# Hybrid decoder layer with a mixture of experts: routing in batches of 4, 2 and 3 tiles, and the overflow tables computed ahead of the first expert rows

## The chip, the cores and the metric

The kernel runs on one core of a Trainium2 chip. The metric is the device time of one launch in microseconds; lower is better. The engines are named as the profile names them: PE (tensor engine, with PEld its weight loads), DVE (vector engine), ACT (scalar engine), POOL (GpSimd) and SP (sync engine, which here only issues DMA).

## The reference, cut to what matters

One layer of a decoder for 1024 prompt tokens and 8 sample tokens, in float32. A mixer (attention, gated spatial unit, dilated attention, pooling) is followed by a norm, and then by the part that the change touches:

```python
def moe(x, w_router, b_router, w1_l, w3_l, w2_l):
    scores = jax.nn.sigmoid(xt @ w_router)
    sel = scores + b_router
    # best group of 4 experts by the sum of its top two, then the top two experts inside it
    ...
    gate = (jax.nn.one_hot(eidx, N_EXPERTS) * gw[..., None]).sum(1)
    for e in range(N_EXPERTS):          # 16
        h = jax.nn.silu(xt @ w1_l[e]) * (xt @ w3_l[e])
        out = out + gate[:, e:e + 1] * (h @ w2_l[e])
```

with x + MoE(x) normed again. Each token goes to two of 16 experts.

## The kernel before, in words

The tokens are nine tiles s = 0 to 8: tile 0 has the 8 sample tokens, tiles 1 to 8 have 128 prompt tokens each. The mixer ends with an output projection of each tile on PE (`y_half`, matmuls of L460 to L462), after which DVE norms it (`normed`, L839 to L852) into `acc`; ACT helps with one square root (L664). SP stores each normed tile to the DRAM array `yd`.

Routing goes in three batches of tiles, `BATCHES`. For a tile, PE transposes the normed rows (`x1_transposes`, recorded at the helper's line L1205), ACT evicts them (`evict_x1T`, L645) and PE multiplies by the router's weights (`logits`, L522). For a batch, ACT takes the sigmoid of all its logits (`scores`, L655 and L657, with another activation table than the square root), DVE picks the two experts of each token (`choose`, L879 to L912; it signals `mask` after L893), PE counts tokens ahead of each token with the same expert (`positions`, L531 and L532), and DVE turns counts into slots (`place`, L921 to L935, which signals `near`). The logits of a batch lie in one of two PSUM banks, batches 0 and 2 in the same.

Each expert owns 128 "near" slots in the DRAM array `xs`. POOL writes rows to them with indirect DMAs (L1056, `slotS`), two for each tile, and waits for `near` of the batch first. Tokens beyond 128 of an expert go to "far" slots, in 16 overflow tiles that are dealt to experts by the counts: `overflow` (L940 to L955, signals `routed`) works out which expert an overflow tile belongs to and whether it is used at all, `far_slots` (L960 to L969 with L931 to L935, signals `far`) the slots, and POOL then scatters again (L1056, `slotO`, 18 more DMAs).

The expert stage runs over 32 tiles q of 128 slots (`QUEUE`: experts 0 to 7, then overflow tiles and experts in turns, then overflow tiles). For a tile SP loads the rows `xg` (L384; for tile 0 it waits until all near scatters have landed, L412), the weights w1 and w3 in two halves m = 2q and 2q + 1 (`w13_raw`, L371), and w2 (L375). The load of w2 for tile 1 waits for `routed`, and everything behind it on SP's queue waits with it. ACT rounds a weight half (`w13_high`, L678) and DVE takes the rest (`w13_low`, L987), so that a float32 product is made of three matmuls. PE does, in this order: `hidden(q+1)` (24 matmuls, L460 to L462, 12 for each weight half), `x_transposes(q+2)` (L1205), `down(q)` (8 matmuls, L593), `h_transposes(q+1)` (L1205). ACT and DVE split the transposed rows (`rows_high` L687, `rows_low` L995 to L1001), make the product of the hidden layer (`silu` L694, `times` L1010) and scale the result by the gates (`out_low` L708, `out_high` L1017). POOL adds the result into `yd` with an accumulating indirect DMA (`add_rows`, L1073). An add starts only when the add before it has landed, and `out_low(q)` and `out_high(q)` wait until add q - 2 has landed. After the last add SP reads `yd` back, and ACT and DVE do the second norm.

Of the kernel before, what the change touches and what calls it, by code (L numbers as in the profile page):

```python
# [24 lines left out]
NT = SEQ // P  # L25
# [40 lines left out]
def build(nc, a):  # L66

    ctx = ExitStack()
    with ctx:
# [166 lines left out]
        WORDER = RORDER  # L236
        BATCHES = ((0, 4), (4, 7), (7, 9))
        DX = D + 4
# [217 lines left out]
        def emit_pe2(pe, mm, tr):  # L456
# [61 lines left out]
            def logits(s):  # L518
                r = rows(WORDER[s])
                pe.wait_ge(S("x1T"), s + 1)  # L520
                for k in range(KD):
                    m = mm(ps[0:r, 6 + batch_of(s) % 2, s * NE:(s + 1) * NE], x1T[:, k, 0:r], wr[:, k, :],  # L522
                           start=(k == 0), stop=(k == KD - 1))
                m.then_inc(S("lg"), 1)
# [13 lines left out]
            for s in range(2, NT + 1):  # L538
# [4 lines left out]
                if s == 7:  # L543
                    pe.wait_ge(S("rc"), 112)
                    positions(0)
            x1_transposes(NT - 1)
            logits(NT - 1)
            positions(1)
            x1_transposes(NT)
# [59 lines left out]
        def emit_act2(act):  # L609
# [50 lines left out]
            for s in range(NT + 1):  # L660
# [6 lines left out]
                if s == 5:  # L667
                    scores(0)
            scores(1)
            evict_x1T(NT - 1)  # L670
# [42 lines left out]
            rows_high(0)  # L713
            rows_high(1)
            silu(0)
            h_evict(0)
            w13_high(3)
            for q in range(NQ):
# [26 lines left out]
        def emit_dve2(dve, link, last_norm):  # L745
# [225 lines left out]
            for s in range(NT + 1):  # L971
# [5 lines left out]
                if s == 6:  # L977
                    place(0)
            choose(1)
            place(1)  # L980
# [39 lines left out]
            w13_low(1)  # L1020
            w13_low(2)
            rows_low(0)
            rows_low(1)
            times(0)
            overflow()
            w13_low(3)
            for q in range(NQ):
                if q + 2 < NQ:
                    w13_low(2 * q + 4)
                if q + 1 < NQ:  # L1030
                    times(q + 1)
                if q + 2 < NQ:
                    rows_low(q + 2)
                    w13_low(2 * q + 5)
                out_high(q)
                if q == 0:
                    far_slots()

# [13 lines left out]
        def emit_pool2(pool):  # L1052
# [24 lines left out]
            for s in range(NT + 1):  # L1077
                for c in range(2):
                    scatter("slotO", s, c, SLOTS - 1, "scat_far")
                if s == 0:  # L1080
                    pool.wait_ge(S("xd"), 16 * (NT + 1))
                if s % 4 == 0:
                    add_rows(s // 4)
            for q in range(3, NQ):
                add_rows(q)
# [1066 lines left out]
```

## Time and profile before

| | |
|---|---|
| median of 3 runs | 1567.37 us (1563.78 to 1569.9) |
| the profiled execution | 1567.51 us, its span 1565.7 us |
| PE busy | 1419.9 us (91%) |
| DVE busy | 743.7 us (47%) |
| ACT busy | 432.2 us (28%) |
| POOL busy | 309.0 us (20%) |
| DMA | 237.70 MB, mean 152 GB/s |

The routing ends and the expert stage begins about three quarters into the span. There are 32 groups of eight matmuls of L593, one for each expert tile, the first at 1195 us. Times in the rows below are microseconds from the span's start. In a timeline a row is one instruction or a run of like ones; the bracket is how long the engine was idle before it and who released it.

### The profile page before, as it was taken

Reading aid. Unit: us, or ns where it says so; the run is one execution under the profiler, and the core shown is the slowest. Engines: PE = TensorE matmul, PEld = TensorE weight load, DVE = VectorE, ACT = ScalarE, POOL = GpSimd, SP = SyncE. Lnnn points to the kernel's source line nnn. Section 1 sums busy time; section 2 is a strip of 40 time slices with the busy share of each in tenths; the row PEclk is TensorE's granted clock in tenths of the full one; section 3 lists DMA queues with packets and bytes.
Section 4 is the critical chain, followed back from the end, with each engine's and each line's share of the span. In section 5 each row is a group of like instructions: output and inputs, shape, how many; then the busy total and the mean of one; then the engine's idle time right before and its main releaser. Section 6 shows DMA issues by size and latency. Waiting matters only on the chain.

```text
span 1565.7 us, 20000 instructions
## 1 busy us (share of the span) xinstructions
PE 1419.9 (91%) x7544; PEld 1068.0 (68%) x7544; DVE 743.7 (47%) x1302; ACT 432.2 (28%) x721; POOL 309.0 (20%) x233
## 2 busy tenths in 40 slices
PE   7999978799998899999999999999938799999980
PEld 3466465444454599999999999878736466666650
DVE  1266445422124442243443444455666466777746
ACT  1111134201015411111111111212124455665536
POOL 1138920045174000000000000000231521221220
PEclk9969999999999999999999999999958899999995
DMA  7346630255331022232222332422376999888645
GB/s 219 104 134 222 207 127 1 71 172 186 132 99 42 35 77 72 77 104 77 73 93 77 106 142 77 145 78 81 120 300 256 312 302 305 289 300 272 202 164 221
DMA packets 75196, 237.70 MB, mean 152 GB/s; under 512 B 17029, under 2 KB 27476, under 8 KB 61422
## 3 DMA queue, kind: packets, MB, share of 16 engines
q1 hardware_dynamic: 48630, 160.73, 28.4%
q0 software_dynamic: 17792, 59.20, 12.8%
q10 hardware_dynamic: 8704, 16.84, 3.1%
q8 instruction: 43, 0.70, 0.2%
q14 instruction: 27, 0.22, 0.0%
HBM read 213.49 MB, written 65.74 MB: 178 GB/s over the span
## 4 chain that ended last, share of the span: by engine, by line
PE 75%; DMA 8%; DVE 6%; POOL 4%; ACT 3%; issue 3%; SPq 0%; POOLq 0%; DVEq 0%; ACTq 0%
PE ps L460 15%; PE ps L462 14%; PE ps L461 14%; PE ps L1224 11%; DMA tmp_yd<-b,b 7%; PE ps L1205 5%; PE ps L593 4%; POOL b L1967 3%; PE ps L1321 2%; PE ps L1358 2%; PE ps L1409 1%; ACT b L1590 1%; PE ps L522 1%; PE ps L1221 1%; PE ps L1239 1%
## 5 line engine op out<-in xcount | busy, mean ns | idle before, releaser
L460 PE MATMUL ps<-b,b 128*128 128x344 f32 (+1 forms) x1360 | 470.3, 346 | 9.3 <-DVE b L987 3.8
L461 PE MATMUL ps<-b,b 128*128 128x344 f32 (+1 forms) x1360 | 465.8, 342 | 0.0
L462 PE MATMUL ps<-b,b 128*128 128x344 f32 (+1 forms) x1360 | 465.8, 342 | 0.0
L460 PEld LDWEIGHTS ps<-b,b 128*128 128x128 f32 x1360 | 255.2, 188 | 30.8 <-issue 10.7
L462 PEld LDWEIGHTS ps<-b,b 128*128 128x128 f32 x1360 | 255.1, 188 | 19.4 <-issue 0.9
L461 PEld LDWEIGHTS ps<-b,b 128*128 128x128 f32 x1360 | 255.0, 188 | 17.0 <-issue 0.6
L1224 PE MATMUL ps<-b,b 128*128 128x512 f32 (+1 forms) x640 | 258.1, 561 | 0.0
L1224 PEld LDWEIGHTS ps<-b,b 128*128 128x128 f32 x640 | 122.3, 194 | 121.7 <-issue 117.1
L1056 POOL DMA_INDIRECT tmp_xs<-b,b x36 | 44.9, 1247 | 634.4 <-issue 574.9
L1205 PE MATMUL ps<-b,b 128*128 128x128 f32 (+1 forms) x782 | 122.8, 286 | 51.0 <-DMA b<-tmp_xs 18.6
L987 DVE TENSOR_TENSOR b<-b,b 128x2048 fp32r<-128x2048 f32 x64 | 146.3, 2289 | 45.3 <-ACT b L678 42.7
L1205 PEld LDWEIGHTS ps<-b,b 128*128 128x128 f32 (+1 forms) x782 | 93.2, 146 | 101.8 <-issue 48.3
L622 ACT ACTIVATE b<-ps,b 128x344 f32<-128x344 f32 x96 | 52.6, 548 | 379.4 <-PE ps L462 379.4
L593 PE MATMUL ps<-b,b 128*128 128x512 f32 x256 | 117.1, 601 | 9.9 <-ACT b L708 9.4
L776 DVE TENSOR_TENSOR b<-b,ps 128x344 f32<-128x344 f32 x72 | 36.9, 513 | 181.8 <-PE ps L462 181.8
L678 ACT CAST b<-b 128x2048 fp32r<-128x2048 f32 x64 | 122.4, 1917 | 0.0
L1073 POOL DMA_INDIRECT tmp_yd<-b,b x32 | 66.2, 2067 | 226.5 <-DMA tmp_yd<-b,b 199.4
L1967 POOL TENSOR_TENSOR b<-b,b 128x2048 f32<-128x2048 f32 (+1 forms) x24 | 87.8, 3657 | 37.2 <-DMA b<-in_state_k 23.0
L593 PEld LDWEIGHTS ps<-b,b 128*128 128x128 f32 x256 | 46.9, 193 | 57.4 <-issue 56.7
L1801 DVE CUSTOM_DVE_ANT_0 b<-ps,b 128x128 f32<-128x128 f32 (+7 forms) x64 | 45.9, 755 | 49.9 <-PE ps L1321 25.1
L1580 ACT ACTIVATE b<-b,b 128x128 f32<-128x128 f32 (+7 forms) x64 | 49.8, 778 | 21.1 <-DVE b L1801 21.1
L1590 ACT COPY b<-ps 128x512 f32<-128x512 f32 (+3 forms) x64 | 32.1, 502 | 78.1 <-PE ps L1205 78.0
(265 smaller groups left out, 1261.9 us busy)
## 6 DMA issues: line engine op xcount, KB each, us to landing
b<-in_w SPq DMA_DIRECT2D x96, 1024.0 KB
b<-in_w_merge SPq DMA_DIRECT2D x32, 640.5 KB, 4.5
tmp_xs<-b ACTq DMA_DIRECT2D x32, 514.0 KB, 4.0
b<-tmp_xs SPq DMA_DIRECT2D x32, 514.0 KB
b<-in_w_in SPq DMA_DIRECT2D x8, 1024.0 KB, 8.6
b<-in_xT SPq DMA_DIRECT2D x4, 1024.0 KB, 12.4
b<-in_w_out SPq DMA_DIRECT2D x4, 1024.0 KB, 7.7
b<-in_x SPq DMA_DIRECT2D x8, 512.0 KB, 4.0
```

Of the source, the lines that this page charges most:

```text
L460: mm(out, hi, mhi, start=start, stop=False)
L461: mm(out, hi, mlo, start=False, stop=False)
L462: return mm(out, lo, mhi, start=False, stop=stop)
L593: m = mm(ps[:, 2 + c, :], hT[:, u, f, :], w2[q % 3][:, f, c * 512:(c + 1) * 512], start=(f == 0), stop=(f == 1))
L622: act.activation(sg[:, j % 2, :], ps[:, (j % 2) * 2, 0:CH], ACT.Sigmoid, bias=bias).then_inc(S("sgd"), 1)
L678: act.copy(w13_hi[m % 3][:].rearrange("p k n -> p (k n)"), w13_raw[m % 4][:].rearrange("p k n -> p (k n)")).then_inc(S("w13h"), 1)
L987: dve.tensor_tensor(lo, raw, hi.bitcast(F32), ALU.subtract).then_inc(S("w13l"), 1)
L1073: pool.indirect_dma_start(a["yd"], bass.IndirectOffsetOnAxis(rt["to"][:, q % 8:q % 8 + 1], 0), yo[:, u, :], None, bounds_check=TOK - 1, oo ...
L1205: return nc.tensor.transpose(out, in_, ident[0:n, 0:n])
L1224: m = mm(ps[:, j % 2, 0:cw], xT[:, k, t * P:(t + 1) * P], w_ring[:, n % 2, k, 0:cw], start=(k == 0), stop=(k == KD - 1))
L1580: act.activation(p_, p_, ACT.Exp, scale=-1.0, bias=am[:, n % 8:n % 8 + 1], accum_out=asum[:, n % 8:n % 8 + 1]).then_inc(S("ex"), 1)
L1967: pool.tensor_tensor(out, k, q, ALU.mult).then_inc(S("kq"), 1)
```

## The change

Six edits. (1) The batches become 4, 2 and 3 tiles in place of 4, 3 and 2. (2) PE does `positions(1)` ahead of the logits of tile 7, and, since tile 6 now shares its PSUM bank with batch 0, waits for `near` of batch 0 before tile 6's logits. (3) ACT takes the scores of batch 1, and DVE does `choose(1)`, after tile 7's norm and ahead of tile 8's. (4) DVE does `overflow` and `far_slots` after the first three weight halves, ahead of `rows_low(0)`. (5) The fourth weight half, m = 3, is split before `silu(0)` and `times(0)`, no more behind them. (6) POOL issues all 18 far scatters before the first add; before, one add stood behind the second and one behind the tenth of them.

```diff
--- before.py
+++ after.py
@@ -234,7 +234,7 @@
         prod = at(BI + 256 + 8 * CH, [P, CH])
 
         WORDER = RORDER
-        BATCHES = ((0, 4), (4, 7), (7, 9))
+        BATCHES = ((0, 4), (4, 6), (6, 9))
         DX = D + 4
 
         wo_raw = [at(OT, [P, KD, 512]), at(XT, [P, KD, 512])]
@@ -518,6 +518,8 @@
             def logits(s):
                 r = rows(WORDER[s])
                 pe.wait_ge(S("x1T"), s + 1)
+                if s == BATCHES[2][0]:
+                    pe.wait_ge(S("near"), 1)
                 for k in range(KD):
                     m = mm(ps[0:r, 6 + batch_of(s) % 2, s * NE:(s + 1) * NE], x1T[:, k, 0:r], wr[:, k, :],
                            start=(k == 0), stop=(k == KD - 1))
@@ -544,8 +546,8 @@
                     pe.wait_ge(S("rc"), 112)
                     positions(0)
             x1_transposes(NT - 1)
+            positions(1)
             logits(NT - 1)
-            positions(1)
             x1_transposes(NT)
             logits(NT)
             positions(2)
@@ -666,7 +668,8 @@
                     merged_high(s + 3)
                 if s == 5:
                     scores(0)
-            scores(1)
+                if s == 7:
+                    scores(1)
             evict_x1T(NT - 1)
             evict_x1T(NT)
             scores(2)
@@ -712,9 +715,9 @@
             w13_high(2)
             rows_high(0)
             rows_high(1)
+            w13_high(3)
             silu(0)
             h_evict(0)
-            w13_high(3)
             for q in range(NQ):
                 if q + 2 < NQ:
                     w13_high(2 * q + 4)
@@ -976,7 +979,8 @@
                     choose(0)
                 if s == 6:
                     place(0)
-            choose(1)
+                if s == 7:
+                    choose(1)
             place(1)
             choose(2)
             place(2)
@@ -1019,11 +1023,12 @@
             w13_low(0)
             w13_low(1)
             w13_low(2)
+            overflow()
+            far_slots()
             rows_low(0)
             rows_low(1)
+            w13_low(3)
             times(0)
-            overflow()
-            w13_low(3)
             for q in range(NQ):
                 if q + 2 < NQ:
                     w13_low(2 * q + 4)
@@ -1033,8 +1038,6 @@
                     rows_low(q + 2)
                     w13_low(2 * q + 5)
                 out_high(q)
-                if q == 0:
-                    far_slots()
 
             def finish(s):
                 r = rows(WORDER[s])
@@ -1077,11 +1080,8 @@
             for s in range(NT + 1):
                 for c in range(2):
                     scatter("slotO", s, c, SLOTS - 1, "scat_far")
-                if s == 0:
-                    pool.wait_ge(S("xd"), 16 * (NT + 1))
-                if s % 4 == 0:
-                    add_rows(s // 4)
-            for q in range(3, NQ):
+            pool.wait_ge(S("xd"), 16 * (NT + 1))
+            for q in range(NQ):
                 add_rows(q)
 
         block = ctx.enter_context(nc.Block())
```

POOL's whole program from the first scatter on. `tmp_xs` is `xs`, `tmp_yd` is `yd`; the second operand of a scatter is `slotS` (b_137664) or `slotO` (b_137760).

```order
-L1056 DMA tmp_xs<-b_99072_151,b_137664_213 4096x1028 x18
-L1056 DMA tmp_xs<-b_99072_151,b_137760_214 4096x1028 x2
-L1073 DMA tmp_yd<-b_82464_170,b_137920_216 1032x1024
-L1056 DMA tmp_xs<-b_99072_151,b_137760_214 4096x1028 x8
-L1073 DMA tmp_yd<-b_82464_170,b_137920_216 1032x1024
-L1056 DMA tmp_xs<-b_99072_151,b_137760_214 4096x1028 x8
-L1073 DMA tmp_yd<-b_82464_170,b_137920_216 1032x1024 x30
+L1059 DMA tmp_xs<-b_99072_151,b_137664_213 4096x1028 x18
+L1059 DMA tmp_xs<-b_99072_151,b_137760_214 4096x1028 x18
+L1076 DMA tmp_yd<-b_82464_170,b_137920_216 1032x1024 x32
```

The two adds that stood between far scatters are now behind all of them.

DVE before, from the third weight half (L987) through `rows_low` of tiles 0 and 1 (L995 to L1001), `times(0)` (L1010) and `overflow` (L940 to L955) to `times(1)`:

```order
L987 TENSOR_TENSOR b_140288_165<-b_0_158,b_24576_162 128x2048
L995 TENSOR_SCALAR b_137920_216<-b_74240_169 128x1
...
L1001 TENSOR_TENSOR b_189440_173<-ps,b_156672_171 128x512 x2
L995 TENSOR_SCALAR b_137920_216<-b_74240_169 128x1
...
L1001 TENSOR_TENSOR b_197136_174<-ps,b_160768_172 128x512 x2
L1010 TENSOR_TENSOR b_187392_178<-b_185344_177,ps 128x256
L940 TENSOR_SCALAR b_137312_209<-b_136672_208 128x16
...
L955 TENSOR_SCALAR b_138016_218<-b_137952_217 128x16
L987 TENSOR_TENSOR b_33024_163<-b_148480_159,b_8192_160 128x2048
L987 TENSOR_TENSOR b_41216_164<-b_168960_156,b_16384_161 128x2048
L1010 TENSOR_TENSOR b_187392_178<-b_185344_177,ps 128x256
```

DVE in the changed kernel, the same stretch; L991 is the weight half, L943 to L958 `overflow`, L963 to L938 `far_slots`, L999 to L1005 `rows_low`, L1014 `times`:

```order
L991 TENSOR_TENSOR b_140288_165<-b_0_158,b_24576_162 128x2048
L943 TENSOR_SCALAR b_137312_209<-b_136672_208 128x16
...
L958 TENSOR_SCALAR b_138016_218<-b_137952_217 128x16
L963 TENSOR_TENSOR b_137504_211<-b_137376_210,b_137312_209 128x16
...
L938 CAST b_137760_214<-b_137568_212 128x2x9
L999 TENSOR_SCALAR b_137920_216<-b_74240_169 128x1
...
L1005 TENSOR_TENSOR b_189440_173<-ps,b_156672_171 128x512 x2
L999 TENSOR_SCALAR b_137920_216<-b_74240_169 128x1
...
L1005 TENSOR_TENSOR b_197136_174<-ps,b_160768_172 128x512 x2
L991 TENSOR_TENSOR b_33024_163<-b_148480_159,b_8192_160 128x2048
L1014 TENSOR_TENSOR b_187392_178<-b_185344_177,ps 128x256
L991 TENSOR_TENSOR b_41216_164<-b_168960_156,b_16384_161 128x2048
```

`overflow` and `far_slots` have moved ahead of the first rows, and one weight half stands ahead of the first `times` (L1014) instead of behind it.

PE at the end of the routing, a piece of the difference; L524 is the logits of a tile, L533 and L534 `positions`, L1205 the transposes.

```order
-L531 MATMUL ps<-b_202384_192,b_193536_182 128x48
-L532 MATMUL ps<-b_202384_192,b_194048_183 128x48
+L533 MATMUL ps<-b_202384_192,b_193536_182 128x32
+L534 MATMUL ps<-b_202384_192,b_194048_183 128x32
+L524 MATMUL ps<-b_206352_150,b_57600_153 128x16 x8
 L1205 MATMUL ps<-b_196624_65,b_99072_151 128x128 x8
-L522 MATMUL ps<-b_206352_150,b_57600_153 128x16 x8
-L531 MATMUL ps<-b_202384_192,b_193536_182 128x32
-L532 MATMUL ps<-b_202384_192,b_194048_183 128x32
+L524 MATMUL ps<-b_206352_150,b_57600_153 128x16 x8
+L533 MATMUL ps<-b_202384_192,b_193536_182 128x48
+L534 MATMUL ps<-b_202384_192,b_194048_183 128x48
```

`positions` of batch 1 (now 32 columns wide, 2 tiles) has moved ahead of tile 7's logits, and that of the last batch is 48 wide.

## Rows read from the trace of the kernel before

**Rows 1.** Timeline, tensor engine, expert tiles: start, us, line, operation, count, [idle before <-releaser].
```profile
1169.34 1.97 PE L1205 MATMUL ps<-b,b 128*128 128x128 f32 x8 [18.59 <-DMA b<-tmp_xs]
...
1181.86 0.44 PE L1205 MATMUL ps<-b,b 128*128 128x128 f32 x2 [0.93 <-DVE b L1010]
...
1188.86 0.77 PE L460 MATMUL ps<-b,b 128*128 128x512 f32 x1 [3.83 <-DVE b L987]
...
1195.02 3.60 PE L593 MATMUL ps<-b,b 128*128 128x512 f32 x8
...
1225.14 3.60 PE L593 MATMUL ps<-b,b 128*128 128x512 f32 x8
...
1245.17 5.47 PE L593 MATMUL ps<-b,b 128*128 128x512 f32 x8 [9.40 <-ACT b L708]
...
1321.42 3.60 PE L593 MATMUL ps<-b,b 128*128 128x512 f32 x8
...
1503.34 3.60 PE L593 MATMUL ps<-b,b 128*128 128x512 f32 x8
```

**Rows 2.** Chain of work that ended last: start, us, what.
```profile
1208.97 13.54 DMA tmp_yd<-b,b
...
1225.12 18.94 DMA tmp_yd<-b,b
...
1251.91 12.85 DMA tmp_yd<-b,b
```

**Rows 3.** Timeline, GpSimd: scatters (L1056) and one add (L1073).
```profile
1155.44 2.43 POOL L1056 DMA_INDIRECT tmp_xs<-b,b  x1 [4.01 <-DVEq L927]
...
1162.58 0.97 POOL L1056 DMA_INDIRECT tmp_xs<-b,b  x1 [0.30 <-issue]
...
1238.05 0.97 POOL L1056 DMA_INDIRECT tmp_xs<-b,b  x1 [0.30 <-issue]
...
1430.52 1.56 POOL L1073 DMA_INDIRECT tmp_yd<-b,b  x1 [10.77 <-DMA tmp_yd<-b,b]
```

**Rows 4.** Two windows: bounds, length, busy us of each engine, clock, DMA share, GB/s.
```profile
1172.00:1188.00 16.00, 12.11 (x46) 9.42 (x46) 8.26 (x31) 6.82 (x7) 0.00 (x0) 0.82 0.06 16
1192.00:1244.00 52.00, 43.64 (x182) 30.40 (x180) 28.76 (x47) 21.10 (x25) 27.98 (x20) 0.93 1.01 382
```

**Rows 5.** Waits of SP's queue from 1160 to 1200: total us, times, longest.
```profile
SPq L375 <- DVEq L956: 19.4, 1, 19.4
```

**Rows 6.** Timeline, vector engine, routing and the first tiles.
```profile
1128.02 1.28 DVE L839 SCALAR_TENSOR_TENSOR b<-b,ps 128x512 f32<-128x512 f32 x2 [3.39 <-PE ps L462]
...
1133.80 0.20 DVE L879 TENSOR_TENSOR b<-b,b 128x48 f32<-128x48 f32 x1
...
1145.73 0.19 DVE L879 TENSOR_TENSOR b<-b,b 128x32 f32<-128x32 f32 x1 [2.52 <-ACT b L657]
...
1154.73 6.70 DVE L987 TENSOR_TENSOR b<-b,b 128x2048 fp32r<-128x2048 f32 x3
...
1169.32 0.15 DVE L995 TENSOR_SCALAR b<-b 128x1 uint32<-128x1 f32 x1 [7.89 <-DMA b<-tmp_xs]
...
1181.72 0.17 DVE L940 TENSOR_SCALAR b<-b 128x16 f32<-128x16 f32 x1
...
1186.43 4.49 DVE L987 TENSOR_TENSOR b<-b,b 128x2048 fp32r<-128x2048 f32 x2
...
1200.61 0.17 DVE L960 TENSOR_TENSOR b<-b,b 128x16 f32<-128x16 f32 x1
...
1204.11 0.18 DVE L935 CAST b<-b 128x18 uint32<-128x18 f32 x1
```

**Rows 7.** Timeline, scalar engine: the square root of the last tile's norm.
```profile
1131.20 0.20 ACT L664 ACTIVATE b<-b 128x1 f32<-128x1 f32 x1 [7.82 <-issue]
```

**Rows 8.** Timeline, tensor engine, routing.
```profile
1133.88 3.59 PE L522 MATMUL ps<-b,b 128*128 128x16 f32 x16 [3.36 <-ACT b L645]
...
1138.73 1.93 PE L1205 MATMUL ps<-b,b 128*128 128x128 f32 x8
```

## The prediction

> **What bounds the kernel now.** I read the timeline of PE first, since PE is 91% busy. From the first expert tile's `down` (1195.02) to the fourth's (1225.14) three tiles take 30.12 us, 10.04 each, without a gap: PE's own pace [rows 1]. By it the fifth `down` is due at 1235.2; it stands at 1245.17, and its row says that PE was idle for 9.40 us, released by ACT's L708, the `out_low` of the tile before [rows 1]. That one waits for add 1 to land, and the chain of waits shows it: add 1 is issued at 1225.12 and takes 18.94 us, to 1244.06 [rows 2]. So from there POOL's adds bound the kernel, until PE has caught them up. `down(29)` is at 1503.34, and 29 tiles at 10.04 would end at 1486.2: the adds, late weights and small gaps cost 17.1 us in all [rows 1].
>
> Why add 1 is late: before it POOL issues ten far scatters, begun only when `far` comes at 1204.3, and add 0 among them, which is issued at 1208.97 and takes 13.54 us [rows 2]; the last scatter is at 1238.05 [rows 3]. Then the windows. From 1172 to 1188 the DMA engines are busy 6% of the time, from 1192 to 1244 more than 100% at 382 GB/s [rows 4]. The idle stretch is one more wait: SP's queue stands for 19.4 us until `routed` (DVE's L956), which sits behind `times(0)` [rows 5].
>
> The second place is PE's restart. It begins at 1169.34 after 18.59 us of waiting for the first rows. It stops again at 1185.03 for 3.83 us, for the weight half m = 3, and the 12 matmuls behind the stop take 5.3 us (1188.86 to 1195.02 less 0.9 for transposes), 0.44 each, where in the steady pace (below) 24 take 5.5: the lower clock level after the higher. So `hidden(1)`, which starts behind `h_transposes(0)` at 1181.86, reaches `down(0)` only at 1195.02 [rows 1].
>
> **Routing tail: later by 3.8 us.** `choose(1)` now stands ahead of tile 8's norm. Norm 7 ends at 1124.63 (1128.02 less 3.39 of idleness) [rows 6]. The choice and placing of a two-tile batch run from 1145.73 to 1154.73, 9.0 us; `choose` has 38 of the 49 instructions, so about 6.9 of it (an estimate). Norm 8 then starts at 1131.5 in place of 1128.02, 3.5 later [rows 6]. The square root, before at 1131.20 [rows 7], comes at 1134.7, and tile 7's eviction can't start before 1134.9. Before it started at 1132.8, as it ended by 1133.88 [rows 8]: plus 2.05. Against that `positions(1)` no longer stands between tile 7's logits and tile 8's transposes: these logits end 3.59 after their start, at 1139.5, and the transposes, before at 1138.73, follow at once, 0.8 later [rows 8]. The last batch has three tiles, whose choice and placing took 9.4 (1133.80 to 1143.2, that is 1145.73 less 2.52) against 9.0: 0.5 with the links. Last `near`: 1.3 late.
>
> POOL has six scatters behind it instead of four. The four span 7.14 us from first start to last, 2.4 each, while three weight halves (L987) run on DVE [rows 3, 6]. Once these are over a scatter takes 0.97 and 0.3 of gap, as the fourth does [rows 3]. I put the two added ones behind them at 1.27: 2.5. Bounds: all six at 1.27 would end the last start 0.8 earlier than before, all at 2.4 would add 4.8. First rows, so: 1.3 + 2.5 = 3.8 late, PE restarts at 1173.1 (range 0.5 to 6.1).
>
> **`overflow` and `far_slots` ahead of the rows: free.** They take 4.7 (1181.72 to 1186.43) and 3.7 us (1200.61 to 1204.3), together 8.4; DVE waits 7.89 for the rows in that very place [rows 6]. With the rows 3.8 later and DVE's start 1.3 later the gap is 10.4: covered, with 2 to spare. Were the rows over 2 us earlier than I think, `rows_low(0)` would be late by the rest. `far` is at about 1171, before 1204.3. `routed` is up at 1167.5, before SP needs it, so w2 of tile 1, rows 2 and 3 and the halves m = 5 and 6, 4.2 MB or 11 us at 382 GB/s, move in the stretch that was idle [rows 4].
>
> **The fourth weight half ahead of `times(0)`: minus 5.6.** ACT splits it when half of `hidden(0)` is done and is over by 1184; DVE's part is 2.25 (two of them take 4.49 [rows 6]) and delays `times(0)` by about 0.9. `h_transposes(0)`: 1181.86 + 3.8 + 0.9 = 1186.6. Then `hidden(1)` runs through at the full level: 24 matmuls are what 10.04 leaves beside 3.6 of `down` and 1.0 of transposes, 5.5 us. With 0.2 ahead and 0.9 of transposes behind `down(0)` is at 1193.2, before 1195.02: minus 1.8 net of the late restart.
>
> **The adds: minus 12.9.** POOL issues 18 far scatters from about 1171.5 on. Before, they and two adds took from 1204.3 to 1239.0, 34.7 us; less the two adds (some 5) about 29.5 [rows 3, 6]. They end at 1201 (at worst, without that allowance, 1206), just after add 0's data. From add 3 (1251.91) to add 20 (1430.52) 17 adds took 178.6 us, 10.5 each, nearly always waiting for the add before [rows 2, 3]. So add 3 comes at 1232.5 instead of 1251.9. `down(q+3)` needs add q landed plus 1.1 (1244.06 to 1245.17). Add q lands at 1201 + 10.5q + 9.8, PE wants `down(q+3)` at 1223.3 + 10.04q: 11.4 us to spare at first, 0.46 less with each add. PE is not held before tile 25, by which time the adds had caught up before too. So the 10.0 us at tile 4 go. Of the rest, 6.0 lie between tiles 4 and 11 (76.25 us for 70.3) and 1.2 between tile 11 (1321.42) and 29 [rows 1]. I keep the last, and half of the 6.0, as waits for weights while the engines are full: 4.2 kept, 12.9 gone (range 7 to 17).
>
> **Sum.** 1567.5 (profiled execution, by 0.1 the median of the runs) - 1.8 - 12.9 = 1552.8; I say 1553. The adds' end and the second norm don't change, nor does anything before 1124. The extra wait before tile 6's logits costs nothing: DVE places batch 0 ahead of norm 7, so `near` is up before PE gets there; only PE's tail is queued behind it. The two more activation table loads fall into ACT's waits (7.82 ahead of the square root [rows 7]).
>
> **Rivals.**
> - *Transfers are the bound.* The engines are full from 1192 on [rows 4], so the stage gains only what moves earlier: 11 us of loads less the restart's 3.8, that is 7, or, by the adds, first add 1201 against 1208.97, 8. Time 1560. For it: the 13.5 and 18.9 us of the first adds fell in the full stretch. Against it: the engines' surplus work is caught up before add 20. Chance 0.27.
> - *Scatters beside DVE's weight halves aren't slowed.* The first of the last four takes 2.43 while L987 runs, the fourth 0.97 after it [rows 3]; if that is chance, six take 7.6, the restart is 0.5 late instead of 3.8, and the time 1549.5. Chance 0.08. The Trainium skill (SBUF - State Buffer, "Who interferes with whom") says that a DVE operation on two tensors has no 2-port mode and didn't stall descriptor generation in its probe, which speaks for this rival; the rows speak against it.
> - *Slower: the first adds land late one after another.* If each takes the mean of the two shown, 16.2, plus 0.7 of issue, the spare 11.4 us shrinks by 6.9 with each, and add 8 lands at 1353: `down(11)` at 1354 where it was 1321.42 [rows 1, 2]. Time 1600. It decides from a mean period over eight adds of 13.3 us. For it: PE pulls more weights while adds are out. Against: add 1 had eight scatters between it and add 0, which now are gone, and periods from add 3 on were 10.5. Chance 0.07. The Trainium skill (DMA: Bandwidth & Descriptors, "Queues, rings and completion order") says that a DMA engine takes turns between its queues packet by packet, which by itself keeps an add from starving behind the weights; no row here shows the turns.
> - *The change doesn't do what it says*: the tail's growth reaches 6 and PE falls to the lower level again between tiles 0 and 1, so only the adds gain, cut to 7: 1563. Chance 0.03.
>
> Mine: 0.55, from 1547 to 1558.
>
> **How the numbers follow.** Half a per cent is 7.8 us, about what a measurement of this kernel can tell from no change. Faster by more: mine and the second, and rather less than half of the first, 0.55 + 0.08 + 0.12 = 0.75. Same: the rest of the first and the last, 0.18. Slower: 0.07. The range of 8 in 10 goes from 1547 to 1562.
>
> **What would show it.** In the changed kernel's trace: norm 8 at 1131.5; last `near` scatter at 1166.4, first rows' transposes at 1173; DVE idle 1 to 3 us ahead of `rows_low(0)`; no wait of SP for `routed`; DMA share above a half from 1175 to 1188; no gap of PE inside `hidden(1)`; `down(0)` at 1193; add 0 at 1201, add 3 near 1233; `down(4)` at 1233.5 without a wait. Add periods over 12, or new waits of PE for weights through tiles 3 to 10, would make me wrong upward; six quick scatters downward.

## The result, and the profile after

The changed kernel takes 1554.03 us (median of 6 runs, 1549.21 to 1558.5), the kernel before, on the same chip, 1564.71 us (1560.5 to 1569.9). The ratio is 0.9931, its 95% interval 0.9904 to 0.9958: faster by 0.7%, or 10.7 us by the medians (6.6 to 15.0 by the interval). The time is inside the predicted range and 1 us from the predicted 1553. That closeness is in part luck: the prediction took 14.7 us off the 1567.5 of the three runs it knew, and over six runs the kernel before stands at 1564.71, so a smaller gain than forecast met a lower start.

| | before | after |
|---|---|---|
| span of the profiled execution | 1565.7 us | 1547.4 us |
| PE busy | 1419.9 us | 1410.2 us |
| POOL busy | 309.0 us | 306.5 us |
| DMA moved | 237.70 MB | 237.70 MB |

The two profiled executions can't be laid on each other as they stand. The first near scatter, which is ahead of everything that the change moves, is this row in the kernel before:

```profile
1119.67 0.96 POOL L1056 DMA_INDIRECT tmp_xs<-b,b  x1 [565.44 <-issue]
```

and this one in the changed kernel, followed by POOL's other scatters (the last six near ones, then some of the 18 far ones) and its first adds (timeline of GpSimd):

```profile
1114.68 0.96 POOL L1059 DMA_INDIRECT tmp_xs<-b,b  x1 [564.18 <-issue]
...
1151.68 2.43 POOL L1059 DMA_INDIRECT tmp_xs<-b,b  x1 [11.68 <-DVEq L930]
1154.42 1.90 POOL L1059 DMA_INDIRECT tmp_xs<-b,b  x1 [0.30 <-issue]
...
1161.38 0.97 POOL L1059 DMA_INDIRECT tmp_xs<-b,b  x1 [0.30 <-issue]
1167.15 0.88 POOL L1059 DMA_INDIRECT tmp_xs<-b,b  x1 [4.80 <-DVEq L972]
...
1179.77 2.56 POOL L1059 DMA_INDIRECT tmp_xs<-b,b  x1 [0.30 <-issue]
...
1191.83 0.97 POOL L1059 DMA_INDIRECT tmp_xs<-b,b  x1 [0.30 <-issue]
1196.71 3.28 POOL L1076 DMA_INDIRECT tmp_yd<-b,b  x1 [3.91 <-DVE b L1021]
1209.38 1.57 POOL L1076 DMA_INDIRECT tmp_yd<-b,b  x1 [9.39 <-DMA tmp_yd<-b,b]
1220.82 1.56 POOL L1076 DMA_INDIRECT tmp_yd<-b,b  x1 [9.88 <-DMA tmp_yd<-b,b]
1232.02 1.86 POOL L1076 DMA_INDIRECT tmp_yd<-b,b  x1 [9.64 <-DMA tmp_yd<-b,b]
```

5.0 of the 18.3 us between the spans are there before the change begins; nothing that the change moves lies ahead of this scatter, and it stands anywhere from 1114.68 to 1123.54 in the twelve traces of this case, so that is variation from run to run. So I count every time from that first near scatter, written t0. From t0 to the end of the span it was 446.0 us and is 432.7: minus 13.3. Each kernel has one trace, so such a difference carries the variation of two single executions; the medians give 10.7. The profiled execution of the kernel before was 2.8 us slower than its median, which would account for the distance, but that the 2.8 lie behind t0 isn't shown. All 18 far scatters are issued before the first add, and add 0 waits for its data (L1021) and no longer stands in a line of scatters [rows 2, 3]. In the chain of work that ended last, the adds' DMAs (`tmp_yd<-b,b`) held 7% of the span before; in the changed kernel they have under 1% of it, at the very end.

The tensor engine, expert tiles (timeline):

```profile
1168.42 1.97 PE L1205 MATMUL ps<-b,b 128*128 128x128 f32 x8 [21.88 <-DMA b<-tmp_xs]
...
1181.88 0.44 PE L1205 MATMUL ps<-b,b 128*128 128x128 f32 x2 [1.93 <-DVE b L1014]
...
1182.62 0.40 PE L462 MATMUL ps<-b,b 128*128 128x512 f32 x1
1182.85 0.59 PE L460 MATMUL ps<-b,b 128*128 128x512 f32 x1
1183.25 0.63 PE L461 MATMUL ps<-b,b 128*128 128x512 f32 x1
...
1190.16 3.60 PE L595 MATMUL ps<-b,b 128*128 128x512 f32 x8
...
1230.37 3.60 PE L595 MATMUL ps<-b,b 128*128 128x512 f32 x8
```

`down(4)`, at 1230.37, stands 40.2 after `down(0)` and has no bracket: the 9.40 us of idleness for L708 are gone [rows 1]. `down(0)` itself comes at t0 + 75.5, where it was t0 + 75.4. Below the first brackets there is something new: a matmul of 512 columns, 0.40 us at first, takes 0.63 from 1183.25 on.

The same in windows (bounds, length, busy us of each engine, clock, DMA share, GB/s):

```profile
1172.00:1188.00 16.00, 14.07 (x50) 11.13 (x49) 6.40 (x6) 6.92 (x7) 12.84 (x11) 0.77 0.86 312
1188.00:1244.00 56.00, 56.00 (x235) 38.51 (x233) 36.48 (x50) 32.32 (x39) 12.15 (x8) 1.00 0.93 342
1182.00:1184.00 2.00, 2.00 (x8) 1.68 (x9) 0.00 (x0) 1.65 (x2) 1.39 (x3) 0.72 0.72 164
1184.00:1186.00 2.00, 2.00 (x6) 1.52 (x6) 1.44 (x1) 0.53 (x1) 1.70 (x2) 0.50 0.96 387
```

The stretch in which the DMA engines were idle [rows 4] is now 86% busy, and SP's wait for `routed` [rows 5] is no longer among its waits. PE has no gap from 1188 to 1244. From 1184 to 1186 the granted clock is 0.50 of full speed, the 1.2 GHz level.

The vector and then the scalar engine between the last batch and `hidden(1)` (timelines):

```profile
1126.59 1.28 DVE L842 SCALAR_TENSOR_TENSOR b<-b,ps 128x512 f32<-128x512 f32 x2
...
1168.40 0.15 DVE L999 TENSOR_SCALAR b<-b 128x1 uint32<-128x1 f32 x1 [2.20 <-DMA b<-tmp_xs]
...
1179.20 2.29 DVE L991 TENSOR_TENSOR b<-b,b 128x2048 fp32r<-128x2048 f32 x1 [4.88 <-ACT b L681]
1181.41 0.41 DVE L1014 TENSOR_TENSOR b<-b,ps 128x256 f32<-128x256 f32 x1
```

```profile
1129.77 0.20 ACT L666 ACTIVATE b<-b 128x1 f32<-128x1 f32 x1 [8.88 <-DVE b L850]
...
1177.26 1.91 ACT L681 CAST b<-b 128x2048 fp32r<-128x2048 f32 x1 [3.67 <-PE ps L462]
1179.18 1.28 ACT L697 ACT_TABLE_LOAD   x1
1180.48 0.38 ACT L697 ACTIVATE b<-ps 128x256 f32<-128x256 f32 x1
```

DVE still waits 2.20 us for the rows after `overflow` and `far_slots`: they cost nothing. But the fourth weight half (L991, 2.29) lies right ahead of `times(0)` (L1014), and PE stands still for 1.93 us until that one is done, where it stood for 0.93. About half of the added 1.0 us comes from ACT. Its part of the half (L681) and the table load behind it (1.28) end at 1180.46, half a us after `hidden(0)`, and hold `silu(0)` up; before, that table load lay in idle time, and `silu(0)` began as `hidden(0)` ended:

```profile
1180.97 0.38 ACT L694 ACTIVATE b<-ps 128x256 f32<-128x256 f32 x1 [5.16 <-PE ps L462]
```

### The profile page after: what moved, and what is told of

It reads as the page before. It is cut to its first block, busy times and chain, and to the rows that moved or that the text cites. A ratio compares the mean times of both kernels' runs of the same rounds, so it can differ in the third digit from the quotient of the medians.

```text
span 1547.4 us, 20002 instructions
## 1 busy us (share of the span) xinstructions
PE 1410.2 (91%) x7544; PEld 1064.3 (69%) x7544; DVE 743.7 (48%) x1302; ACT 435.6 (28%) x723; POOL 306.5 (20%) x233
## 2 busy tenths in 40 slices
DMA packets 75197, 237.70 MB, mean 154 GB/s; under 512 B 17030, under 2 KB 27477, under 8 KB 61423
## 4 chain that ended last, share of the span: by engine, by line
PE 79%; DVE 6%; DMA 6%; ACT 4%; POOL 3%; issue 2%; SPq 0%; POOLq 0%; DVEq 0%; ACTq 0%
PE ps L460 15%; PE ps L462 15%; PE ps L461 15%; PE ps L1224 11%; PE ps L595 6%; PE ps L1205 5%; PE ps L1321 2%; PE ps L1358 2%; DMA b<-in_w 2%; POOL b L1967 2%; DMA b<-in_cache_k,b 2%; PE ps L1409 1%; PE ps L524 1%; ACT b L1590 1%; PE ps L1239 1%
## 5 line engine op out<-in xcount | busy, mean ns | idle before, releaser
L991 DVE TENSOR_TENSOR b<-b,b 128x2048 fp32r<-128x2048 f32 x64 | 146.4, 2290 | 64.1 <-ACT b L681 63.9
L1205 PE MATMUL ps<-b,b 128*128 128x128 f32 (+1 forms) x782 | 122.2, 285 | 55.0 <-DMA b<-tmp_xs 21.9
L1205 PEld LDWEIGHTS ps<-b,b 128*128 128x128 f32 (+1 forms) x782 | 93.0, 146 | 105.0 <-issue 48.8
L681 ACT CAST b<-b 128x2048 fp32r<-128x2048 f32 x64 | 122.2, 1913 | 27.2 <-DMA b<-in_w 23.6
```

The lines of the kernel that those rows point to most:

```text
L681: act.copy(w13_hi[m % 3][:].rearrange("p k n -> p (k n)"), w13_raw[m % 4][:].rearrange("p k n -> p (k n)")).then_inc(S("w13h"), 1)
L991: dve.tensor_tensor(lo, raw, hi.bitcast(F32), ALU.subtract).then_inc(S("w13l"), 1)
L1205: return nc.tensor.transpose(out, in_, ident[0:n, 0:n])
```

## The experiments

The theory that these traces suggest: the gain is the adds' (edits 4 and 6), edits 1 to 3 cost some 4 us at PE's restart, and edit 5 wins little, because PE's stop before `h_transposes(0)` is longer and the clock falls after it. All places below are starts, in us from t0 of the same trace, and each is from one trace. A ratio is to the runs of the kernel before on the same chip beside that kernel (medians 1562.2 to 1565.0).

| kernel | down(0) | add 0 | down(29) | median us | ratio to before, interval |
|---|---|---|---|---|---|
| before | 75.4 | 89.3 | 383.7 | 1564.71 | |
| changed | 75.5 | 82.0 | 370.5 | 1554.03 | 0.9931, 0.9904 to 0.9958 |
| edit 6 alone | 75.2 | 114.2 | 389.4 | 1572.18 | 1.0066, 1.0038 to 1.0094 |
| edit 4 alone | 72.6 | 79.2 | 379.3 | 1561.99 | 0.9988, 0.9969 to 1.0006 |
| edits 1 to 3 undone | 71.4 | 81.0 | 369.1 | 1554.59 | 0.9932, 0.9918 to 0.9946 |
| edit 5 undone | 77.1 | 83.6 | 371.8 | 1555.61 | 0.9960, 0.9941 to 0.9979 |
| tables ahead of the halves | 71.8 | 78.4 | 366.6 | 1549.45 | 0.9914, 0.9884 to 0.9944 |
| silu ahead of half 3 | 73.8 | 80.3 | 369.6 | 1551.62 | 0.9919, 0.9902 to 0.9937 |
| three batches kept: tables first, half 2 behind `rows_low(1)`, silu ahead of half 3 | 70.4 | 77.0 | 365.9 | 1549.44 | 0.9918, 0.9901 to 0.9935 |
| all four: the same, with batches back | 67.0 | 77.8 | 364.5 | 1548.57 | 0.9895, 0.9878 to 0.9913 |
| changed, small w2 | 75.0 | 81.6 | 366.6 | 1549.72 (one run) | |
| edits 1 to 3 undone, small w2 | 71.6 | 81.1 | 363.1 | 1550.95 (one run) | |

**Edit 6 alone** (the kernel before, all far scatters ahead of the adds).

```diff
-                if s == 0:
-                    pool.wait_ge(S("xd"), 16 * (NT + 1))
-                if s % 4 == 0:
-                    add_rows(s // 4)
-            for q in range(3, NQ):
+            pool.wait_ge(S("xd"), 16 * (NT + 1))
+            for q in range(NQ):
                 add_rows(q)
```

> The kernel before, with only the adds moved behind all 18 far scatters (edit 6 alone). Theory A (dates of the adds hold PE): the scatters still begin at 1204 of the trace of before and take some 29.5 us, so add 0 goes out near 1234 and lands near 1245; down(3), which was at 1225.1, comes at about 1246, and with adds every 10.5 us the stage never makes that good before tile 20. Time 1574 to 1585, slower. Theory B (the DMA engines' throughput holds PE): the same bytes in the same stretch, weights run ahead while the adds wait; 1562 to 1569, no change.

Slower by 0.7%, as theory A says, and a little under the 1574 to 1585 us that it gave. With `far` still late, POOL begins its 18 far scatters at 1206.19 and does add 0 behind the last:

```profile
1206.19 2.24 POOL L1056 DMA_INDIRECT tmp_xs<-b,b  x1 [41.55 <-DVEq L969]
...
1233.71 0.97 POOL L1056 DMA_INDIRECT tmp_xs<-b,b  x1 [0.30 <-issue]
1234.99 1.59 POOL L1073 DMA_INDIRECT tmp_yd<-b,b  x1 [0.31 <-issue]
1241.65 1.57 POOL L1073 DMA_INDIRECT tmp_yd<-b,b  x1 [5.07 <-DMA tmp_yd<-b,b]
1248.42 3.18 POOL L1073 DMA_INDIRECT tmp_yd<-b,b  x1 [5.20 <-DMA tmp_yd<-b,b]
```

`down(3)` waits 15.77 us for L700. The size was smaller than expected: adds 0 and 1 have 6.7 and 6.8 us to the next where they have 12.7 and 11.4 in the changed kernel. The likely reason is that a stalled PE asks for fewer weights (DMA share 0.42 from 1235 to 1248); no run here varies that alone.

**Edit 4 alone** (the kernel before, with `overflow()` and `far_slots()` ahead of `rows_low(0)`).

```diff
             w13_low(2)
+            overflow()
+            far_slots()
             rows_low(0)
             rows_low(1)
             times(0)
-            overflow()
             w13_low(3)
...
-                if q == 0:
-                    far_slots()
```

> The kernel before, with only overflow and far_slots moved ahead of the first rows (edit 4 alone; batches, the fourth weight half and POOL's order as before). Theory A: far scatters begin near 1167, add 0 is not held, the 10 us gap at tile 4 goes, and 12 to 13 us come off: about 1552, with the later stop inside hidden(1) kept. DVE is at most 0.6 us late for the first rows. Rival: it is the order on POOL (edit 6) that counts, since eight scatters still stand between adds 0 and 1, and the gain is half or less: 1558 or more.

No gain that the measurement can tell. The rival, POOL's order, is right:

```profile
1172.07 0.88 POOL L1055 DMA_INDIRECT tmp_xs<-b,b  x1 [7.15 <-DVEq L969]
1173.26 0.87 POOL L1055 DMA_INDIRECT tmp_xs<-b,b  x1 [0.31 <-issue]
1200.19 3.27 POOL L1072 DMA_INDIRECT tmp_yd<-b,b  x1 [26.06 <-DVE b L1017]
1203.77 1.01 POOL L1055 DMA_INDIRECT tmp_xs<-b,b  x1 [0.30 <-issue]
```

Two scatters go, then add 0 heads the queue, waits 26.06 us for its data, and holds the other 16 scatters back into the stretch in which the DMA engines are full. From t0 to `down(29)` edit 4 alone gives 4.4 us, edit 6 alone costs 5.8, and the whole change gives 13.2: the adds' gain needs both. (No run has exactly edits 4 and 6; the two below, with edits 1 to 3 or edit 5 undone, have both and keep the gain.) Of the 4.4 us, 2.8 are there at `down(0)`: `overflow` no longer stands between `times(0)` and the fourth weight half on DVE, and PE's stop inside `hidden(1)` is 1.96 us instead of 3.83. So edit 4 helps the restart too, which the prediction gave to edit 5 alone.

**Edits 1 to 3 undone** (the changed kernel with the batches and the order of `positions(1)`, `scores(1)` and `choose(1)` of before, and without the wait for `near`).

```diff
-        BATCHES = ((0, 4), (4, 6), (6, 9))
+        BATCHES = ((0, 4), (4, 7), (7, 9))
...
-                if s == 7:
-                    choose(1)
+            choose(1)
```

> The changed kernel with batches of 4, 3 and 2 tiles again and tile 7's logits ahead of positions (edits 1, 2 and 3 undone). Counted from the first near scatter, the changed kernel's PE restarts 4.1 us later than before's. Theory A: that is the price of these three edits (1.2 for the later last near signal, 2.5 for two more scatters, the rest landing), so the restart is 4 sooner, down(0) and down(29) too, and the time is 1550 against 1554. Rival: DVE has the tables (8.4 us) in a gap that is 7.9 again, is late for the first rows, and eats 2 or more of the 4: 1552 or later. Rival 2: weights for tiles 5 to 8 absorb it: down(11) and the end move less than 1.5.

The same time as the changed kernel, where 3 to 4 us less were expected. The trace agrees with the first half of the argument: `down(0)` is 4.0 us earlier. But `down(29)` is only 1.4 earlier, the size that rival 2 gave. The waits from 1200 to 1310 (total us, times, longest) show who takes it back:

```profile
ACT b L708 <- DMA tmp_yd<-b,b: 22.5, 8, 5.8
ACT b L678 <- DMA b<-in_w: 14.1, 7, 3.6
DVE b L1017 <- DMA tmp_yd<-b,b: 5.2, 4, 2.8
```

and in the changed kernel, same stretch:

```profile
ACT b L681 <- DMA b<-in_w: 22.3, 9, 4.4
ACT b L711 <- DMA tmp_yd<-b,b: 8.6, 3, 4.1
DVE b L1021 <- DMA tmp_yd<-b,b: 2.3, 2, 1.7
```

Add 0 moved by 1.1 us only (81.0 for 82.0), since `far` moved little. With PE 4.0 earlier ACT's `out_low` (L708) waits for adds again, 22.5 us for 8.6, and the weight halves queued behind it on ACT are late. The adds' DMAs are back in the chain that ended last, with 6% of the span. So it is the adds that take it back, and not, as rival 2 had it, the weights alone.

**Edit 5 undone** (the changed kernel with `w13_high(3)` behind `h_evict(0)` and `w13_low(3)` behind `times(0)`).

```diff
-            w13_high(3)
             silu(0)
             h_evict(0)
+            w13_high(3)
```

> The changed kernel with the fourth weight half split behind silu(0) and times(0) as before (edit 5 undone). Theory A (each us of the restart counts): the stop before h_transposes(0) shrinks from 1.93 to 0.93, the one of 3.8 inside hidden(1) is back with the lower clock behind it, down(0) comes about 3.4 us later against norm 8 and the time is 1557. Rival (weights hold tiles 5 to 8 anyway): the later start is absorbed there, down(11) is at most 1 us later, time 1554 to 1555.

`down(0)` is 1.6 later and `down(29)` 1.2: edit 5 is worth no more than that, less than the 3.4 expected, and in the times the intervals overlap. How much of the 1.6 is the edit's this trace can't say: `silu(0)` started 2.3 us after the matmuls that it waits for, for a reason that the trace doesn't name ("remote").

```profile
1186.44 0.38 ACT L697 ACTIVATE b<-ps 128x256 f32<-128x256 f32 x1 [7.24 <-remote]
```

Two other traces give a figure without that disturbance. Edit 4 alone and edits 1 to 3 undone differ in edits 5 and 6, and the adds of edit 6 come after `down(0)`: 72.6 against 71.4, so edit 5 is worth 1.2 us there.

**Tables ahead of the halves** (the changed kernel, DVE works out `overflow` and `far_slots` first).

```diff
+            overflow()
+            far_slots()
             w13_low(0)
             w13_low(1)
             w13_low(2)
-            overflow()
-            far_slots()
```

> The changed kernel with overflow and far_slots ahead of the three weight halves on DVE instead of behind them. Theory P (a running weight half of DVE slows POOL's indirect DMAs): the six last near scatters take 0.97 each instead of 2.43, 1.90, 1.90, 0.97 and so on, the last starts 3.3 us sooner, PE restarts 3.3 sooner, far scatters follow at once and some of them are slowed instead; time 1551 if the restart counts in full. Rival Q (the slow ones are chance or come from the idle time before them): the first scatter still takes over 2 us and the restart moves by less than 1. Rival R: restart sooner but absorbed by late weights of tiles 5 to 8: 1554.

This settles the six near scatters. With small operations on DVE beside them the near ones take their short time, and the far ones, which now meet the halves, the long one:

```profile
1156.77 0.97 POOL L1059 DMA_INDIRECT tmp_xs<-b,b  x1 [11.65 <-DVEq L930]
...
1165.88 2.24 POOL L1059 DMA_INDIRECT tmp_xs<-b,b  x1 [1.70 <-issue]
1168.43 1.90 POOL L1059 DMA_INDIRECT tmp_xs<-b,b  x1 [0.31 <-issue]
```

PE restarts 3.6 us sooner, and in the trace it counts in full: `down(0)` 3.7 and `down(29)` 3.9 sooner. Here add 0 moved by 3.7 too (78.4), unlike with edits 1 to 3 undone. The ratios, 0.9914 against 0.9931, aren't told apart.

**silu ahead of half 3** (the changed kernel; the half is still ahead of `h_evict(0)`).

```diff
-            w13_high(3)
             silu(0)
+            w13_high(3)
             h_evict(0)
```

(and `times(0)` ahead of `w13_low(3)` on DVE.)

> The changed kernel with silu(0) and times(0) ahead of the fourth weight half on ACT and DVE, but that half still ahead of h_evict(0) and of everything else. Theory A: the stop of PE ahead of h_transposes(0) falls from 1.93 to 0.93, a stop of 0.8 comes in inside hidden(1), and the fall to the lower clock level that followed the 2.3 us stop (1.7 us lost) may go: down(0) 1 to 2.5 us sooner, counted from the first near scatter, time 1552. Rival: the lower level comes all the same (it came after a stop of 2.3 us and might after 1.3): nothing gained, 1554.

PE has two short stops in place of a long one, the granted clock is 1.00 of full speed (2.4 GHz) from 1182 to 1188, and `down(0)` is 1.7 sooner (timeline of PE):

```profile
1181.85 0.44 PE L1205 MATMUL ps<-b,b 128*128 128x128 f32 x2 [0.93 <-DVE b L1014]
...
1184.68 0.40 PE L462 MATMUL ps<-b,b 128*128 128x512 f32 x1
1185.60 0.47 PE L460 MATMUL ps<-b,b 128*128 128x512 f32 x1 [0.52 <-DVE b L991]
1185.91 0.40 PE L461 MATMUL ps<-b,b 128*128 128x512 f32 x1
```

At `down(29)` 0.9 of it are left; the times can't show so little.

**All four** (the changed kernel with edits 1 to 3 undone, tables first, the third weight half's `w13_low(2)` behind `rows_low(1)`, silu first; the piece on DVE).

```diff
+            overflow()
+            far_slots()
             w13_low(0)
             w13_low(1)
-            w13_low(2)
-            overflow()
-            far_slots()
             rows_low(0)
             rows_low(1)
-            w13_low(3)
+            w13_low(2)
             times(0)
+            w13_low(3)
```

> Four things together on the changed kernel: batches of 4, 3 and 2 again, tables ahead of the weight halves on DVE, the third half (m = 2) behind rows_low(1), silu(0) ahead of the fourth. Theory A: 4.1 from the batches, 3.3 from quick scatters, 1 from silu: down(0) 8 us sooner than in the changed kernel counted from the first near scatter, time 1546. Rival: weights hold the tiles up to 10, since loads don't start sooner than the rows are read, and half of it is absorbed: 1550.

1548.57 us, the lowest median of all: 1.05% under the kernel before. Its interval (0.9878 to 0.9913) still overlaps that of the changed kernel (0.9904 to 0.9958). `down(0)` is 8.4 sooner than in the changed kernel, as expected, and `down(29)` 6.0: between theory A, which keeps all of it, and the rival, which keeps half.

**Three batches kept** (as the run before, but edits 1 to 3 stay; the piece on the batches, against the run before).

```diff
-        BATCHES = ((0, 4), (4, 7), (7, 9))
+        BATCHES = ((0, 4), (4, 6), (6, 9))
```

> The changed kernel with its batches of 4, 2 and 3 kept, but the tables ahead of all three weight halves, and silu(0) and times(0) ahead of the fourth half. It differs from the run with all four mends only in edits 1 to 3. All counted from the first near scatter. Theory A (PE's restart sets the end once the adds are early enough, and the adds set it otherwise): down(0) is that of the tables-first run, +71.8, less the 1.8 us of the lower clock level, so +70.0; add 0 at +78; the adds, not moved by silu, hold PE again through tiles 5 to 10, so that down(29) is between +364.5 and +366.6, and the batches cost 0 to 2 us of the 3 that they delay the restart. Time 1549 to 1551, ratio 0.990 to 0.992. Theory B (everything behind the restart moves with it): down(29) at +364.5 + 3.0 = +367.5 or later, time 1551.5, ratio 0.992 to 0.993.

As theory A says. `down(0)` is at 70.4, 3.4 later than with the batches back, and `down(29)` at 365.9, 1.5 later: once more less than half of the restart's delay reaches the end. In the times 0.9918 against 0.9895 isn't told apart, as the intervals overlap.

**Small w2** (the changed kernel; for tiles 3 on only one eighth of w2 is loaded, so the output isn't the layer's).

```diff
+                if q < 3:
+                    sp.dma_start(w2[q % 3][:].rearrange("p k n -> p (k n)"), src, ...)
+                else:
+                    sp.dma_start(w2[q % 3][:].rearrange("p k n -> p (k n)")[:, 0:256], src[:, 0:256], ...)
```

> The changed kernel, with w2 loaded in full for tiles 0 to 2 only and to one eighth for all others, so that the results of the experts are wrong by the old weights left in the buffer: 0.9 MB less of some 4.2 for each tile. Theory B (the transfers make tiles 5 to 8 take 10.9 to 11.3 us instead of 10.04): these tiles take 10.04 to 10.1, adds land sooner (periods of 9 instead of 11.4), down(29) comes 3.3 us sooner against down(0), and that is all, since PE's own pace holds the rest. Rival (it is the adds' latency or ACT's order): the tiles stay at 10.8 and more.

PE has no wait at all from tile 0 to 29: 291.5 us for 29 tiles, 10.05 each, where the changed kernel takes 295.0. Window from 1192 to 1304:

```profile
1192.00:1304.00 112.00, 112.00 (x471) 78.47 (x470) 79.74 (x99) 66.44 (x78) 28.82 (x15) 1.00 0.85 268
```

So the 3.5 us (0.8 to 1.3 in each of the three steps from `down(5)` to `down(8)`) are the transfers'. The adds come faster as well, 10.1 us apart over the first eight where the changed kernel has 11.8, though not at the 9 expected.

**Edits 1 to 3 undone, small w2** (the changed kernel with both, so its output isn't the layer's either; the piece on the batches).

```diff
-        BATCHES = ((0, 4), (4, 6), (6, 9))
+        BATCHES = ((0, 4), (4, 7), (7, 9))
```

> The run with edits 1 to 3 undone, and w2 loaded only to one eighth for tiles 3 on, so that its output isn't the layer's. One look for the places of the groups. With the batches back down(0) came 4.0 us sooner than in the changed kernel (+71.4 from the first near scatter against +75.5), but down(29) only 1.4 sooner. Theory A (the give-back is the work of the full DMA engines: adds and weights come at their pace, not at PE's): with less to load nothing is given back, down(0) at +71.4 and down(29) at +71.4 + 291.5 = +362.9, 3.6 before the small-w2 run's +366.55. Theory B (POOL's add chain starts only 1.1 us sooner, whatever the transfers do): down(29) at +366.55 - 1.4 = +365.1, with ACT and DVE waiting for adds.

As theory A says, with less to load the restart's gain is kept whole, although add 0 moved by only 0.5 us. `down(0)` 71.6, `down(29)` 363.1, 3.5 sooner than with small w2 alone.

## Why the prediction was right, point by point

The sign and the larger term, the adds', were right, and by the cause that was given. The sum was 14.7 us of gain; the traces have 13.3 from t0 on and the medians 10.7.

**The adds: minus 12.9, measured minus 13.3.** From `down(0)` to `down(29)` it was 308.3 us and is 295.0. Add 0 was predicted at 1201 on the clock of before (its times are 4.99 above those of the changed kernel's trace) and came at 1201.7 (1196.71 + 4.99). Here two misses cancel: the far scatters took 25.6 us from first start to end, not 29.5, and were over before add 0's data, while those data were later than predicted, as `down(0)` was by 2 us. The adds then took longer than the 10.5 us each that I read from the later ones: 12.7, 11.4, 11.2, 12.1, so add 3 was at t0 + 117.3, 4.5 us late by my step. "Add periods over 12" was named as a sign of being wrong upward, and three of the first eight were over 12; the 11.4 us to spare paid for them, and PE waited for none of it through tile 4. What is kept of the waits for weights is 3.9, predicted 4.2. Edit 6 and edit 4 by themselves show that the step was a joint one: scatters early and adds behind them. What moved is the bound: with the adds out of the chain that ended last until its end, it is made of PE and, at tiles 5 to 8, of the weights' loads.

**Routing tail: later by 3.8, measured 4.1.** Norm 8 at 1131.6 on the clock of before (predicted 1131.5), square root 1134.8 (1134.7), last near scatter 1166.4 (1166.4), restart 1173.4 (1173.1). That it is edits 1 to 3 is shown by undoing them: `down(0)` 4.0 sooner. What the prediction didn't see is that this delay costs only 1.4 us at the end, because the adds, stretched by the full DMA engines, stand right behind PE.

**Tables free.** Right: 2.2 us of waiting left, predicted 2. A gain lay there, though: ahead of the halves they let six near scatters run quick. Their move also took `overflow` from between `times(0)` and the fourth half, worth 2.8 us at `down(0)` by edit 4 alone.

**The fourth half: minus 1.8, measured plus 0.1.** This is the term that was mis-sized: minus 5.6 by itself, less 3.8 for the late restart. With edits 1 to 3 undone it is minus 3.9 (75.4 to 71.4), of which edit 4 gives 2.8 and edit 5 1.2. `h_transposes(0)` came at 1186.9, predicted 1186.6. The step that failed is "then `hidden(1)` runs through at the full level": PE stood 1.93 us ahead of these transposes, 1.0 us after they began the granted clock fell to 0.50, stayed there for 3.4 us, and the 24 matmuls took 7.2 us, not 5.5. The prediction had counted the 0.9 us by which the half delays `times(0)`, and not that it makes the stop longer. (The expectation of the silu run puts this stop at 2.3 us, counted from the start of the last matmul ahead of it; the bracket has 1.93.) In the twelve traces the lower level, seen as matmuls that take up to 0.63 us where others take 0.40, goes with the longer stops. There is one trace of each kernel, so it isn't shown that every execution does the same:

| stops of PE between hidden(0) and down(0), us | first slowed matmul | kernels |
|---|---|---|
| 0.93, then 3.82 to 3.83 | at the end of the second stop | before, edit 6 alone |
| 0.93, then 1.96 | 0.3 us behind the second | edit 4 alone |
| 1.92 to 1.94 | 0.5 to 1.0 us behind it | changed, edits 1 to 3 undone, tables ahead, both with small w2 |
| 3.15, then 0.73 | at the end of the first | edit 5 undone |
| 0.93, then 0.52 to 0.58 | none | silu ahead of half 3, three batches kept, all four |

**The rivals.** *Transfers are the bound*: not at the end, since 13.3 were gained and not 7 or 8. In part it holds: 3.5 us of the stage are theirs (small w2), and they stretch the adds, which is what takes back a sooner restart. *Scatters aren't slowed*: refuted. The Trainium skill (SBUF - State Buffer, "Who interferes with whom") tells of a probe that found no stall of descriptor generation beside a DVE operation on two tensors; here an indirect DMA takes 1.90 to 2.43 us beside L991 and 0.97 to 1.01 when L991 is moved away. The same section of the Trainium skill also says that a DVE instruction with two inputs in SBUF contends with a GpSimd instruction that reads SBUF, which the prediction left out; these times agree with that, and no run shows which port or step it is. *Slower, adds one after another late*: the first eight periods came to 11.8 on average, the longest 13.4, short of the mean of 13.3 from which it decides. With edit 6 alone the kernel did get slower, by another way: an add that starts too late. *The change doesn't do what it says*: its one half, the lower level between tiles 0 and 1, happened; the other didn't.

**What stays open**: the 2.3 us ahead of `silu(0)` with edit 5 undone, and whether the batches of 4, 2 and 3 cost time in the median; the traces say 1.4 to 1.5 us, which is below what the medians can tell. Open too is how much of the 13.3 us of the two traces is the change's, where the medians have 10.7.

## What to carry to other kernels

When two chains run side by side, here PE's tiles and POOL's adds, a gain on one counts only up to the distance to the other; the run that moved both by 3.7 us kept all of it, and the one that moved PE by 4.0 and the adds by 1.1 kept 1.4. The distance is not fixed by the first add alone: with less to load, PE moved by 3.5 and add 0 by 0.5, and all 3.5 were kept, since the adds then came faster. And moving both by 1.7, with silu ahead of half 3, kept 0.9. An in-order queue that serves two streams has to be reordered together with what makes the first stream ready; each half alone gave nothing that the medians can tell, or cost time. Ahead of a first tile, put the work that PE waits for ahead of the work that it needs next, even when the second is larger: two stops of 0.9 and 0.5 us cost less than one of 1.9.

## What the runs showed of the hardware

- GpSimd is busy for 0.87 to 1.01 us with an indirect DMA to `xs`, and mostly for 1.9 to 2.6 us (up to 3.08) when a `TENSOR_TENSOR` of 128x2048 from float32 to fp32r runs on DVE; small DVE operations (128x16 to 128x256) beside the six near scatters didn't slow them.
- It is not that operation alone. In all twelve traces the third and fourth near scatter take 1.85 or 1.86 and 1.19 or 1.20 us beside a `SCALAR_TENSOR_TENSOR` of 128x1024. All 99 of the 432 scatters that took over 1.1 us overlap one of the two operations; of the others, the 303 that meet neither took 0.87 to 1.01, and the 30 that overlap one had begun before it, or in one case 0.04 us after.
- Stops of PE of 1.92 to 1.94 us were followed by the 1.2 GHz level 0.5 to 1.0 us after PE had begun again, for some 3.4 us (five kernels); stops of 0.93 and then 0.52 to 0.58 us, some 3 us apart, weren't (three kernels).
- From one accumulating indirect DMA of 128 rows to the next, each waiting for the one before, it was 6.7 and 6.8 us where the DMA engines were 42% busy (edit 6 alone, 1235 to 1248), and 11.2 to 12.7 where they were 93% busy at 342 GB/s (changed, 1188 to 1244). The busy share alone doesn't set it: with small w2 it was 9.9 to 10.9 at the same 93%, but 307 GB/s (1200 to 1244).
